# Inverting a triangular matrix from 32-row blocks in place of 16-row blocks: a longer solve on VectorE, one joining level less on TensorE

## The reference

```python
m = jnp.where(strict, bc[..., None] * kk * decay, 0.0)
lhs = m + jnp.eye(CHUNK, dtype=f32)
rhs = jnp.concatenate([vc * bc[..., None], kc * (bc * jnp.exp(gcum))[..., None]], axis=-1)
sol = lax.linalg.triangular_solve(lhs, rhs, left_side=True, lower=True, unit_diagonal=True)
u, w = sol[..., :A_DV], sol[..., A_DV:]
def step(S, inp):
    q_c, k_c, u_c, w_c, g_c, qk_c = inp
    v_new = u_c - jnp.einsum('bhcd,bhde->bhce', w_c, S)
    o = (jnp.einsum('bhcd,bhde->bhce', q_c * jnp.exp(g_c)[..., None], S)
         + jnp.einsum('bhcs,bhse->bhce', qk_c, v_new))
    S = (S * jnp.exp(g_last)[..., None, None] + jnp.einsum('bhcd,bhce->bhde', ..., v_new))
```

## Time and profile before

| | |
|---|---|
| median of 3 runs | 2940.18 us (2939.53 to 2942.92) |
| the profiled execution's own time | 2939.03 us |
| its span in the profile | 2937.2 us |
| PE busy | 2880.9 us (98%) |
| DVE, ACT, POOL busy | 1478.0, 985.3, 1371.3 us (50, 34, 47%) |
| mean granted TensorE clock | 0.994 |
| the solve of the first of the two layers | starts at 1405.32 us, its transposed copy at 1416.04 us |

### The profile page before, as it was taken

One profiled execution on the slowest core, in us unless ns is written; L12 is line 12 of the kernel. 1 busy time (PEld: TensorE's weight loads), 2 busy tenths in 40 slices (PEclk: granted clock), 3 DMA queues, 4 the chain that ended last, 5 costly groups with the idle time before them and its releaser, 6 DMA issues.

```text
span 2937.2 us, 46243 instructions
## 1 busy us (share of the span) xinstructions
PE 2880.9 (98%) x18790; PEld 2580.3 (88%) x18790; DVE 1478.0 (50%) x2412; ACT 985.3 (34%) x1470; POOL 1371.3 (47%) x1748
## 2 busy tenths in 40 slices
PE   9999999999999999999899999999999899999999
PEld 6778888877888889888799999999989799999999
DVE  6955322276532227995444544234897545444241
ACT  3453222245322233333343322224343434322221
POOL 5426555555655455432125555456442214555454
PEclk9989999999999999999999999999999999999999
DMA  5203332322333333322324222323322413323322
GB/s 176 65 22 102 99 96 92 100 93 66 100 100 94 93 98 118 100 67 85 105 69 132 87 89 92 94 85 96 102 73 73 114 62 113 105 91 93 95 89 70
DMA packets 124632, 271.25 MB, mean 92 GB/s; under 512 B 22808, under 2 KB 59032, under 8 KB 124184
## 3 DMA queue, kind: packets, MB, share of 16 engines
q1 hardware_dynamic: 73104, 246.05, 26.5%
q10 hardware_dynamic: 51336, 22.41, 2.8%
HBM read 250.35 MB, written 18.07 MB: 91 GB/s over the span
## 4 chain that ended last, share of the span: by engine, by line
PE 90%; DVE 5%; ACT 2%; issue 1%; ACTq 1%; DMA 0%; POOL 0%; DVEq 0%; POOLq 0%
PE acc L647 68%; PE acc L1023 5%; PE aux L1037 4%; PE acc L696 3%; PE acc L1004 2%; PE aux L1004 2%; DVE conv_out L2016 1%; PE acc L1233 1%; PE aux L864 1%; PE acc L680 1%; PE aux L909 1%; PE acc L1037 1%; PE aux L819 0%; PE aux L891 0%; PE acc L755 0%
## 5 line engine op out<-in xcount | busy, mean ns | idle before, releaser
L620 POOL TENSOR_TENSOR w_lo<-w_raw,w_hi 128x256 fp32r<-128x256 f32 x1744 | 1371.1, 818 | 1549.0 <-ACT w_hi L1267 1548.6
L647 PE MATMUL acc<-n_hi,w_hi 128*128 128x264 f32 (+1 forms) x3072 | 776.5, 314 | 5.4 <-POOL w_lo L620 3.8
L647 PE MATMUL acc<-n_lo,w_hi 128*128 128x264 f32 (+1 forms) x3072 | 767.6, 312 | 0.0
L647 PE MATMUL acc<-n_hi,w_lo 128*128 128x264 f32 (+1 forms) x3072 | 765.5, 311 | 0.0
L1267 ACT ACTIVATE w_hi<-w_raw 128x1024 fp32r<-128x1024 f32 (+1 forms) x436 | 455.0, 1044 | 701.0 <-PE acc L647 625.1
L647 PEld LDWEIGHTS acc<-n_hi,w_hi 128*128 128x128 f32 x3072 | 502.7, 188 | 57.0 <-issue 15.3
L647 PEld LDWEIGHTS acc<-n_lo,w_hi 128*128 128x128 f32 x3072 | 500.8, 188 | 34.4 <-issue 2.6
L647 PEld LDWEIGHTS acc<-n_hi,w_lo 128*128 128x128 f32 x3072 | 500.6, 188 | 31.3
L2118 DVE TENSOR_TENSOR x<-x,acc 128x512 f32<-128x512 f32 (+1 forms) x144 | 100.1, 695 | 571.2 <-PE acc L647 524.8
L647 PE MATMUL acc<-hidden_lo,w_hi 128*128 128x264 f32 (+1 forms) x1216 | 345.3, 331 | 0.0
L647 PE MATMUL acc<-hidden_hi,w_hi 128*128 128x264 f32 (+1 forms) x1216 | 345.2, 331 | 0.0
(11 more groups left out here) (477 smaller groups left out, 3761.2 us busy)
## 6 DMA issues: line engine op xcount, KB each, us to landing
w_raw<-in_stream SPq DMA_DIRECT2D x420, 512.0 KB, 3.5
unit_blocks<-unit_scratch ACTq DMA_DIRECT2D x30, 256.0 KB, 4.5
w_raw<-in_stream SPq DMA_DIRECT2D x16, 384.0 KB, 3.1
unit_scratch<-unit_staged ACTq DMA_DIRECT2D x20, 256.0 KB, 2.8
saved_x<-x SPq DMA_DIRECT2D x2, 2112.0 KB, 8.6
x<-saved_x SPq DMA_DIRECT2D x16, 264.0 KB, 2.7
saved_gates<-root ACTq DMA_DIRECT2D x12, 264.0 KB, 2.1
unit_scratch<-unit_staged ACTq DMA_DIRECT2D x1, 2560.0 KB, 13.3
```

The source lines that it names most:

```text
L620: i = pool.tensor_tensor(wl[:, slot, s], raw[:, slot, s], wh[:, slot, s].bitcast(F32), ALU.subtract)
L647: last = pe.matmul(o, w[:, p % W_SLOTS, P * b:P * b + P], r, start=(b == 0 and i == 0), stop=(b == n - 1 and i == 2))
```

## The change

The solve works on 32x32 blocks. There are 64 of units 1 to 4 and 4 of unit 0, and they now lie in 68 partitions of one tile. The substitution has 31 columns. After 22 of them (`SOLVE_BREAK`) the piece z0 is taken, which before was taken after the solve. The solved blocks lie in `squares`, their transpose in `unit_b`, the products in a tile of their own. Since `squares` is cleared next, VectorE waits for `solved_sent` ahead of the two clears. The joining has two levels. In each slot with a join, `step_out(v)` now stands between `join(u, 0)` and `join_half(u, 1)`, and the FILL table deals the same 48 blocks differently: 12, 7, 7, 7, 7, 8 for the slots in place of 8 for each.

```diff
-FILL = [[8, 0, 0, 0, 0, 0, 0]] + [[1, 1, 1, 2, 1, 1, 1]] * 4 + [[2, 1, 2, 0, 0, 0, 3]]
+FILL = [[8, 4, 0, 0, 0, 0, 0], [1, 1, 1, 1, 1, 2, 0], [1, 1, 1, 1, 1, 2, 0], [1, 1, 1, 1, 1, 1, 1], [1, 1, 1, 1, 1, 2, 0],
+        [2, 1, 2, 0, 0, 0, 3]]
...
-SMALL = 16
-LEVELS = (4, 5, 6)
+SMALL = 32
+LEVELS = (5, 6)
+LAST = len(LEVELS) - 1
+SOLVED = 4 * A_HEADS * (P // SMALL)
+SOLVES = SOLVED + A_HEADS
+SOLVE_BREAK = 22
...
+            if v >= 0:
+                step_out(v)
             if joined:
                 join_half(u, 1)
             fill(FILL[s][4])
             if joined:
                 join(u, 1)
-            if v >= 0:
-                step_out(v)
-            if joined:
-                join_half(u, 2)
             fill(FILL[s][5])
-            if joined:
-                join(u, 2)
             fill(FILL[s][6])
...
-            act.dma_start(lt[0:A_HEADS, 1, :, :], small_blocks(M_PART, 0)).then_inc(blocks_landed, 16)
-            act.dma_start(lt[:, 0, :, :], small_blocks(M_PART, 1)).then_inc(blocks_landed, 16)
+            act.dma_start(lt[SOLVED:SOLVES, :, :], small_blocks(M_PART, 0)).then_inc(blocks_landed, 16)
+            act.dma_start(lt[0:SOLVED, :, :], small_blocks(M_PART, 1)).then_inc(blocks_landed, 16)
...
-                    if m == 5:
-                        dve.wait_ge(solved_sent, 64 * (l + 1))
...
             attention(l, filler)
+            dve.wait_ge(solved_sent, 64 * (l + 1))
             step(dve.memset(decayed, 0.0))
...
             for j in range(SMALL - 1):
+                if j == SOLVE_BREAK:
+                    between()
                 n = SMALL - 1 - j
-                shape = [P, 2, n, j + 1]
-                rows, t = solved[:, :, j + 1:, 0:j + 1], products[:, :, 0:n, 0:j + 1]
+                shape = [SOLVES, n, j + 1]
+                rows = solved[0:SOLVES, j + 1:, 0:j + 1]
+                t = products[0:SOLVES, 0:n * (j + 1)].rearrange("p (n c) -> p n c", n=n)
...
+            dve.wait_ge(bo_ready, 5 * (l + 1))
...
-            solve_blocks(l)
-            filler(*ATTN_FILLERS[7])
+            solve_blocks(l, lambda: filler(*ATTN_FILLERS[7]))
```

More of the change, by code:

```diff
@@ L378, in build @@
     ik = rest.take("index_k", [P, T])
+    bv = rest.take("attn_v", [P, T])
     bk = rest.take("attn_k", [P, T])
-    bv = rest.take("attn_v", [P, T])
     selb = rest.take("select_bias", [P, SEL_AT[4]])
@@ L390, in build @@
     meta_p = rest.take("meta_probs", [P, B_HEADS, META])
+    products = rest.take("solve_products", [P, SMALL * SMALL // 4])
     glast = rest.take("chunk_decay", [P, UNITS, A_HEADS])
@@ L405, in small_tiles @@
     def small_tiles(a):
-        return a[:, 0:2 * SMALL * SMALL].rearrange("p (s r c) -> p s r c", s=2, r=SMALL)
+        return a[:, 0:SMALL * SMALL].rearrange("p (r c) -> p r c", r=SMALL)
     states = [four(ssq[:, :]), four(sqb[:, 0, :])]
@@ L415, in build @@
     dt = [four(ub[:, 0, :]), four(ub[:, 1, :])]
-    lt, solved, turned, products = small_tiles(ik[:, :]), small_tiles(rt[:, :]), small_tiles(ub[:, 1, :]), small_tiles(bv[:, :])
+    lt = Area(nc, W + 3 * TILES4, end).take("solve_blocks", [P, SMALL, SMALL])
+    solved, turned = (small_tiles(a[:, :, :].rearrange("p s t -> p (s t)")) for a in (sqb, sb_))
     gates = [ub[:, 0, :], ub[:, 1, :], sb_[:, 0, :], sb_[:, 1, :]]
@@ L425, in small_blocks @@
     def small_blocks(kind, u):
-        n, step = (P, 1) if u else (A_HEADS, P // SMALL)
+        n, step = (SOLVED, 1) if u else (A_HEADS, P // SMALL)
         return bass.AP(scratch, kind * KIND_PITCH + u * UNIT_PITCH, [[step * BLOCK_PITCH, n], [P, SMALL], [1, SMALL]])
@@ L1077, in join @@
                 pe.wait_ge(vb_ready, c.next(vb_ready, A_HEADS))
-            if n < 2:
+            if n < LAST:
                 heads(aux[:, 0, :], lambda o, h: mm_(o, y_in[:, h, :], p1[:, h, :]))
@@ L1755, in send_solved @@
             for part, t in ((X_PART, solved), (Y_PART, turned)):
-                act.dma_start(small_blocks(part, 0), t[0:A_HEADS, 1, :, :]).then_inc(solved_sent, 16)
-                act.dma_start(small_blocks(part, 1), t[:, 0, :, :]).then_inc(solved_sent, 16)
+                act.dma_start(small_blocks(part, 0), t[SOLVED:SOLVES, :, :]).then_inc(solved_sent, 16)
+                act.dma_start(small_blocks(part, 1), t[0:SOLVED, :, :]).then_inc(solved_sent, 16)
         def fetch_unit(u, parts=(M_PART, X_PART, Y_PART)):
@@ L1800, in slot @@
             gap(4)
-            gap(5)
-            if joined:
-                half(aux[:, 0, :])
             if v >= 0:
@@ L1819, in slot @@
                 out_roots()
+            gap(5)
             gap(6)
@@ L2713, in slot @@
                 join_block(1)
-                join_block(2)
             gap(2)
@@ L2721, in slot @@
             gap(4)
[L2722 to L2725, removed]
             if v >= 0:
@@ L2757, in normalise @@
                     .then_inc(bp_ready, c.made(bp_ready))
-            step(dve.memset(ik[:, SMALL * SMALL:2 * SMALL * SMALL], 0.0))
             dve.wait_ge(bs_full, c.next(bs_full))
```

15 lines of the change are left out of this document (8 added, 7 removed).

## The result

The changed kernel takes 2945.65 us (median), against 2940.02 us before: a ratio of 1.0018, 95% interval 1.0011 to 1.0025, so some 5 us slower (3.2 to 7.4). Two of its 20 executions took 3998 and 7257 us; the ratio goes by the other 18, whose median is 2945.18 us. The profiled execution took 2942.43 us; its span is 2940.6 us.

The account below looks back on a forecast made before the run. TensorE, busy 98% of the span, was taken as the bound. The longer solve loses 20.6 us and one level less wins 12.6, so 8.0 us slower: median 2948, with 2938 to 2955 held at some 8 in 10.

Parts of the forecast that it names:

- The gain: Slots 1 to 4, one join level less: 6.3 us won a layer, 12.6 us for both, after new waits.
- The waits ahead of `step_out` and of `w_and_u(2)`: TensorE in slots: about 1.5 us ahead of `step_out` in slots 3 and 4, 1.0 in slot 2; 2.5 ahead of `w_and_u(2)`.
- the one behind the take of gate2-6: Slot 3: the block at place 6 waits for VectorE's last subtraction and take, 1.15 us more.
- The loss: Longer solve and its HBM round trip ahead of `w_and_u(0)`: 11.1 us first layer, 9.5 second, 20.6 together.
- my formula: Solve steps on VectorE: each costs 0.19 us plus 1.1 ns for each element; 62 steps take 23.8 us.
- I take 7.4 us for both: Sending solved blocks, first send to first fetch: 7.4 us in both layers, since the number of rows is the same.
- my first rival: The send is short: 2.5 of its 7.4 us came from tiles queued ahead; 2943; chance 0.2, shared with full clock.
- three of the four blocks at 1.39: TensorE's gate2-5 blocks after the second idleness: three at the lower clock, one at 0.74, 4.9 us in all.
- z1 and the transposes are done at about 1435.3: TensorE in slot 0: both finish then, before the second wait, for the sent blocks, which ends at 1442.7.
- costs nothing by itself: TensorE's first idleness, ahead of z1 (start 1426.5 in place of 1418.98), is free because the second wait ends later.
- The rule that was weighed: Sending 128-byte rows: 7 cycles a descriptor in place of 5, up to 3 us more a layer, near 2954.
- The rival of no new waits: Slots with a join have no new waits: 13.3 us won a layer, 6 us faster, 2934; chance 0.12.

Follow-up runs that it names:

- both_orders: Changed kernel with two VectorE reorderings: output-bank copy ahead of the first join's subtractions, inverse's last subtraction ahead of the output's mean; 2929.07 us, ratio 0.9964.
- fill_12_more: all_orders_fill with solved-block transfers issued ahead of the transposed copy and four more z2 blocks in slot 0, other slots' blocks redealt; 2917.46 us, ratio 0.9925.
- after_tiles_ahead: Changed kernel with the megabyte of tiles fetched right ahead of the sends instead of 15 us earlier; 2953.16 us, ratio 1.0047.
- short_solve: Changed kernel without the solve's first 19 columns (result not the inverse), z0 taken behind the copy; 2923.24 us, ratio 0.994.
- break14: Changed kernel with z0 taken after 14 columns of the solve in place of 22; 2944.33 us, ratio 1.0019.
- copy_first: Changed kernel with VectorE's copy that frees the output bank placed ahead of the first join's two subtractions; 2936.84 us, ratio 0.9988.
- all_orders_fill: both_orders with state cleared and z1 taken ahead of the wait for sent blocks, four more blocks in slot 0; 2929.19 us, ratio 0.9968.

## Why the prediction was right

**The direction and its reason hold.** The level's gain lies in the slots, the loss is the solve with its trip through HBM, and the loss is larger. By the profiles, up to `step_v(4)`, the two layers are 5.0 us longer (2.4 and 2.6), by the medians 5.6. Predicted were 8.0. The loss was forecast 4.8 us too large for both layers, the gain 1.8 us too large. That the two errors partly cancel in the total is luck. By the prediction's own threshold of 0.2% (2946.1 us) the median lies just inside no change, which it gave 0.33.

**The gain** was predicted at 6.3 us a layer and measured at 6.17 and 4.63. With the moved blocks counted, slots 1 to 4 of the first layer are shorter by 4.19, 0.88, 1.43 and 2.62 us (from `step_v` to `step_v`); my terms with them are 4.24, 0.69, 1.59 and 2.74. The second layer lost 1.3 us in slot 2 to the clock, which I had not counted. The waits ahead of `step_out` and of `w_and_u(2)` were each shown by an experiment of its own; the one behind the take of gate2-6 (0.96 us) is a row that stays in both_orders and goes when fill_12_more moves the block behind it.

**The loss** was predicted at 11.1 and 9.5 us and measured, at `step_v(0)` and less the moved blocks, at 8.56 and 7.23. The solve was 1.0 us shorter than worked out: its 256-element steps stand 0.455 us apart, 0.47 by my formula. The terms that were mis-sized are two. "I take 7.4 us for both" for the send was 1.6 us too much, and my first rival had the reason: before, the send stood behind the tiles. I gave it 2 in 10, and held against it that the second layer took 0.8 us longer in the same order; but in after_tiles_ahead and short_solve, with the tiles close again, the second layer is longer too (by 0.3 and 0.6 us), and without them it isn't (5.74 against 5.81), so that difference goes with the tiles as well. And "three of the four blocks at 1.39" was 1.3 us too much: the four took 3.57 us, since part of the stretch at the lower clock was spent on the transposes.

**A step was wrong in its place.** I wrote that z1 and the transposes are done at about 1435.3, ahead of the second wait. The transposes need the cleared state, so they stood behind that wait too. The take of z1 ends at 1438.47 and the blocks start at 1439.60, 1.0 us later than with my 0.14 us between them. The order of the waits would have told it: `slot(0)` waits for `state_ready` ahead of `tokens(0)`. That the first idleness "costs nothing by itself" was right, as break14 shows.

**The rule that was weighed** does not show. The Trainium skill, DMA: Bandwidth & Descriptors, section "Why small descriptors are slow (HBM only)", would make the send of 128-byte rows up to 3 us longer. The trace doesn't agree. Without the tiles ahead 128-byte rows moved for 3.6 us and 64-byte rows for 3.2, and over the whole lag the difference is 1.4 us at most; with them ahead it is 7.7 to 8.6 us against 7.4 and 8.2. The sum by the number of rows was the better one, though not exact.

**The rival of no new waits** was wrong for this kernel, and right for what the level is worth: it said 13.3 us a layer, and both_orders has 13.06.

## What to carry to other kernels

When a step is taken off the busiest engine, look up what stood behind it in the other engines' queues: here two orders on VectorE hid more than half of the gain, though in the kernel before TensorE has no wait at either place, and mending them turned 5.6 us slower into 11 us faster. When an engine must wait for a fixed round trip, first ask what can be put in front of it: idleness there cost the same wherever it stood (to within 1 us), and work there was free until it filled the wait. Where TensorE was busy up to the end of the wait, it also kept its clock (1.05 us for the group in fill_12_more, 2.05 in all_orders_fill). Before you take the duration of a transfer from a trace, look at what was issued ahead of it in the same queue.

## What the runs showed of the hardware

- The time of many small writes went with what was issued ahead of them in the queue far more than with the length of the row. From first send to fetch it was 5.7 to 5.95 us without a megabyte of fetches right ahead and 7.4 to 8.6 us with it, for 64 and 128 bytes alike. The issue of the third send shows it on its own: 0.85 to 0.92 us, or 2.4 to 3.25 us, in kernels that issue the four in a row.
- The 2112 or 2176 rows of each of two tiles moved, first layer, in 3.2 us as 64-byte rows (some 83 GB/s) and in 3.6 us as 128-byte rows (some 148 GB/s).
- After almost the same idleness the clock did not come back after the same time. In after (6.40 us idle) the matmul pairs are at 0.41 us 2.95 us after the restart. In copy_first (6.51 us idle) they are at 0.40 only 6.1 us after it, with a granted clock of 0.50 from 1442.0 to 1448.5, and `w_and_u(0)` starts 1.4 us later for it:

```profile
1442.47 1.09 PE L1066 MATMUL aux<-const,delta_k 128*128 128x128 f32 x4 [6.51 <-issue]
...
1448.16 0.58 PE L1030 MATMUL acc<-n_hi,w_hi 128*128 128x264 f32 x2
1448.58 0.40 PE L1030 MATMUL acc<-n_lo,w_hi 128*128 128x264 f32 x2
```

- A wait of 2.1 us ahead of `w_and_u(2)` was followed by the lower clock in some cases (2.08 us for the group) and not in others (1.16), even in the two layers of one execution of after. What decides it is open.
